# Attention on Trainium2: row maxima from 64-row tile pairs, latent scores in 2.5 passes, half the low-part subtractions on GpSimd

## The chip, the cores and the metric

One core of one Trainium2 chip runs the whole layer as one program. The time is the device time in microseconds of one execution, as the median of several runs. All times below are of this core.

## The reference

The layer is h = x + W_out(concat[GQA(xn) * silu(g_A), MLA(xn) * silu(g_B)]) with xn = RMSNorm(x), for 2048 tokens of width 1024, in float32. Both mixers are bidirectional softmax attention over all 2048 keys:

```python
def one_block(qblk):
    s = jnp.einsum('bkgqd,bksd->bkgqs', qblk, k).astype(jnp.float32) * scale
    p = jax.nn.softmax(s, axis=-1).astype(v.dtype)
    return jnp.einsum('bkgqs,bksd->bkgqd', p, v)
```

GQA has 8 query heads and 2 key/value heads of dimension 64. The latent mixer (MLA) has 4 heads with keys of 96 (64 + 32 rotary) and values of 128. Queries and keys are RMS-normalised per head, with gains about eight times the usual, so scores are large and softmax is sharp: the row maximum must be taken off before exp.

## The kernel before

The program has three phases: phase1 (projections, norms, rotary, transposes; up to 598 us), phase2 (attention; up to about 1636 us) and phase3 (gates and output projection). The change touches phase2 alone.

Float32 accuracy comes from float16 pairs: every operand is a high half and a low half (what float16 leaves over). A score tile is a sum of products of halves, accumulated in PSUM. For GQA (64 dimensions) the high and the low half of a key lie in partitions 0 to 63 and 64 to 127 of ka_hl, and qa_hh holds the high half of the query twice, so one matmul gives high x (high + low); a second one (ka_h1, qa_lm, 66 rows) adds high key x low query and, through two more rows, takes off the row maximum. For latent heads (96 dimensions) it takes three matmuls (L1026 to L1028).

**Units and steps.** Queries come in blocks of 512. phase2 runs N = 16 rounds; a round has three units: a GQA unit of key head 0, a GQA unit of key head 1 and a latent unit (UNITS, L700), each 512 queries against all 2048 keys. A unit has STEPS = 8 steps of 256 keys, a round HALF = 24 steps. A step s does:
- PE: two score tiles of 128 keys x 512 queries into st[:, s % 2] (scores, L1005 to L1029).
- ACT: exp of the 1024 columns into p32 (L847, float32), then its float16 high half ph (L852). p32 has N32 = 4 slots, ph and pl have NP = 8.
- DVE: the low half pl = p32 - ph (lo, L891 to L897).
- PE: P V of the step three earlier (PVLAG = 3; pv, L1033 to L1061), high and low half of P against the values, into acc. The values carry a column of ones, which gives the denominator.

**Row maxima ahead.** The row maximum of a unit must be there before its first score. So PE computes the scores twice: once with queries in rows (128 queries x 512 keys, max_scores, L962 and L964, high halves; GQA with the key's low half as well), into one of the two banks of mx; DVE reduces them (reduce, L869), one bank or both at a time; sixteen such pieces make a unit. Then DVE reduces the partial maxima and splits them in two float16 numbers (max_done, L873 to L879), PE turns them into a row by a product with the unit matrix (turn, L975 to L981, output 2 columns wide), and DVE casts that row into the query operand (rows, L886, L888). The pieces run LEAD = 30 ahead of the scores; a hand-written list (PIECES_IN, L637) says how many of them each step carries (48 in a round), and PE puts them between its scores and its P V halves. A prologue does the first 30 before the first score.

**Ends of units.** ACT copies acc to acc_sb (copy_acc, L839) at the third step of the next unit, DVE takes the reciprocal of the denominators (L912) two steps on, and GpSimd (POOL) adds the two GQA halves (L818) and multiplies by the reciprocal (L827). SP stores the result and loads the operands (L729 to L801) in one queue: queries of the next round after each unit's scores (s_st), the latent max operands after the round's row maxima (s_mx), latent keys after the last scores, latent values after the last P V (s_pv).

PE's order within a step is fixed by the program: scores, then max pieces and turn, then P V. The waits that tie the engines are: scores s wait for exp s - 2; exp s waits for the subtraction s - 4; a max piece waits until the piece before the last is reduced (L958); P V waits for ph and pl of its step.

Of the kernel before, what the change touches and what calls it, by code (L numbers as in the profile page):

```python
# [19 lines left out]
F16 = mybir.dt.float16  # L20
ALU = mybir.AluOpType
# [3 lines left out]
P = 128  # L25
# [11 lines left out]
QB = 512  # L37
# [588 lines left out]
def phase2(nc, QA, KA, QBd, KBd, VA, VB, YA, YB, w_out, w_raw):  # L626
# [8 lines left out]
    PIECES_IN = [2, 2, 2, 0, 2, 2, 2, 0] + [2, 2, 0, 2, 2, 2, 0, 2] + [2, 3, 3, 3, 3, 2, 4, 4]  # L637
    ROUND = 3 * PIECES
    pieces_of = lambda s: list(range(LEAD + sum(PIECES_IN[:s]), LEAD + sum(PIECES_IN[:s + 1])))
    KW = 2 * QB  # L640
    ONE = 64.0
    with ExitStack() as ctx:
# [19 lines left out]
        part = sb("part", [P, 2, PIECES])  # L662
# [21 lines left out]
        s_mx = sem("max_scores")  # L684
        s_red = sem("max_reduced")
# [6 lines left out]
        s_lo = sem("p_lo")  # L692
# [13 lines left out]
        def turned(s, last):  # L706


            for e in pieces_of(s - 1) if s else ():
                if e % PIECES == 3 and not (last and e // PIECES > 3):  # L710
                    return e
            return None

        def before(i, s, act_on, first):

            pos = s // STEPS - 1
            act_on(i if pos >= 0 else i - 1, pos % 3, first and pos == 0)
# [10 lines left out]
        def _(sp):  # L728
            def load_q(i, pos):  # L729
# [34 lines left out]
            for g in range(GA):  # L764
                for s, dsts in ((0, (ka_hl[g][0:64, :], ka_h1[g][0:64, :])), (1, (ka_hl[g][64:128, :],))):
# [586 lines left out]
```

## Time and profile before

| | us |
|---|---|
| median of 3 runs | 1847.05 |
| lowest, highest | 1846.85, 1848.38 |
| span of the profiled execution | 1847.9 |
| busy: PE, DVE, ACT, POOL | 1672.5, 1333.0, 1167.0, 61.6 |
| attention phase, first max matmul to last copy | 606.2 to 1633.3 |

The profile is of one execution, whose own time is given by its span alone. PE is TensorE (matmuls), PEld its weight loads, DVE VectorE, ACT ScalarE, POOL GpSimd, SP the queue that issues DMAs. Ends of matmuls are modelled, so start-to-start distances say more of PE than busy time. "Idle before" is the engine's idle time ahead of a row and what released it. The granted TensorE clock (PEclk) is a share of 2.4 GHz.

### The profile page before, as it was taken

Reading aid. Unit: us, or ns where it says so; the run is one execution under the profiler, and the core shown is the slowest. Engines: PE = TensorE matmul, PEld = TensorE weight load, DVE = VectorE, ACT = ScalarE, POOL = GpSimd, SP = SyncE. Lnnn points to the kernel's source line nnn. Section 1 sums busy time; section 2 is a strip of 40 time slices with the busy share of each in tenths; the row PEclk is TensorE's granted clock in tenths of the full one; section 3 lists DMA queues with packets and bytes.
Section 4 is the critical chain, followed back from the end, with each engine's and each line's share of the span. In section 5 each row is a group of like instructions: output and inputs, shape, how many; then the busy total and the mean of one; then the engine's idle time right before and its main releaser. Section 6 shows DMA issues by size and latency. Waiting matters only on the chain. (4 is left out here: it accounts for less than half of the span.)

```text
span 1847.9 us, 39666 instructions
## 1 busy us (share of the span) xinstructions
PE 1672.5 (91%) x14416; PEld 1003.5 (54%) x14416; DVE 1333.0 (72%) x1829; ACT 1167.0 (63%) x1506; POOL 61.6 (3%) x92
## 2 busy tenths in 40 slices
PE   4599999999994499999999999999999999959999
PEld 2355555555553056656665666666656665634444
DVE  4644545445463599999999999999999999842332
ACT  5445444454443088778877877887788778953332
POOL 0000000000000000000000000000000000000000
PEclk8799999999997599999999999999999999979999
DMA  6312302212221802212221222122212221235553
GB/s 215 108 46 65 95 32 82 77 51 77 63 71 52 209 23 62 68 44 53 58 68 36 62 57 65 35 68 57 65 31 72 57 61 34 54 100 165 173 174 126
DMA packets 202876, 143.54 MB, mean 78 GB/s; under 512 B 43216, under 2 KB 186064, under 8 KB 202832
## 3 DMA queue, kind: packets, MB, share of 16 engines
q1 hardware_dynamic: 202832, 142.94, 27.6%
q8 instruction: 29, 0.48, 0.1%
q14 instruction: 15, 0.12, 0.0%
HBM read 100.94 MB, written 41.97 MB: 77 GB/s over the span
## 5 line engine op out<-in xcount | busy, mean ns | idle before, releaser
L847 ACT ACTIVATE p_p<-p_st 128x1024 f32<-128x1024 f32 x384 | 390.2, 1016 | 210.5 <-PE p_st L1028 127.1
L869 DVE TENSOR_REDUCE p_part<-p_mx 128x1 f32<-128x512 f32 (+1 forms) x564 | 479.7, 878 | 38.0 <-PE p_mx L962 33.0
L896 DVE TENSOR_TENSOR p_pl<-p_p,p_ph 128x1024 f16<-128x1024 f32 x384 | 466.6, 1222 | 13.5 <-ACT p_ph L852 11.6
L515 PE MATMUL p_ring<-p_w_hi,p_xT 128*128 128x512 f16 (+3 forms) x1536 | 393.4, 343 | 34.2 <-issue 18.9
L852 ACT ACTIVATE p_ph<-p_p 128x1024 f16<-128x1024 f32 x384 | 405.8, 1057 | 16.6
L515 PE MATMUL p_ring<-p_w_lo,p_xT 128*128 128x512 f16 (+3 forms) x768 | 263.3, 343 | 0.0
L515 PEld LDWEIGHTS p_ring<-p_w_hi,p_xT 128*128 128x128 f16 x1536 | 152.1, 99 | 154.5 <-issue 42.8
L962 PE MATMUL p_mx<-p_ka_hl,p_qa_hh 128*128 128x512 f16 x512 | 190.3, 397 | 49.9 <-DVE p_part L869 28.5
L1053 PE MATMUL p_acc<-p_vas,p_ph 128*128 128x129 f16 x2048 | 219.7, 221 | 15.0 <-ACT p_acc_sb L839 15.0
L1054 PE MATMUL p_acc<-p_vas,p_pl 128*128 128x65 f16 x2048 | 211.0, 193 | 0.0
L1053 PEld LDWEIGHTS p_acc<-p_vas,p_ph 128*128 128x128 f16 x2048 | 183.6, 97 | 44.8 <-ACT p_acc_sb L839 22.9
L1054 PEld LDWEIGHTS p_acc<-p_vas,p_pl 128*128 128x128 f16 x2048 | 182.3, 98 | 29.0
L1024 PE MATMUL p_st<-p_qa_lm,p_ka_h 66*128 66x512 f16 x512 | 195.2, 381 | 0.0
L1023 PE MATMUL p_st<-p_qa_hh,p_ka_hl 128*128 128x512 f16 x512 | 194.8, 380 | 0.0
L1057 PE MATMUL p_acc<-p_vbs,p_ph 128*128 128x129 f16 x1024 | 184.9, 219 | 1.6 <-ACT p_acc_sb L839 1.6
L1059 PE MATMUL p_acc<-p_vbs,p_pl 128*128 128x129 f16 x1024 | 185.3, 222 | 0.0
L1058 PE MATMUL p_acc<-p_vbs,p_ph 128*128 128x128 f16 x1024 | 184.8, 219 | 0.0
L1302 PE MATMUL p_po<-p_w_hi,p_yT 128*128 128x512 f16 x512 | 159.0, 383 | 9.9 <-DVE p_res L1252 5.4
L962 PEld LDWEIGHTS p_mx<-p_ka_hl,p_qa_hh 128*128 128x128 f16 x512 | 48.0, 98 | 127.7 <-DVE p_part L869 90.7
L393 DVE COPY p_xT<-p_xtp 128x1024 f16<-128x1024 f16 x32 | 20.7, 686 | 133.4 <-PE p_xtp L539 133.4
L1057 PEld LDWEIGHTS p_acc<-p_vbs,p_ph 128*128 128x128 f16 x1024 | 100.9, 99 | 15.5 <-ACT p_acc_sb L839 2.1
L1058 PEld LDWEIGHTS p_acc<-p_vbs,p_ph 128*128 128x128 f16 x1024 | 98.7, 96 | 16.7
(136 smaller groups left out, 2158.2 us busy)
## 6 DMA issues: line engine op xcount, KB each, us to landing
p_vbs<-scratch_vb SPq DMA_DIRECT2D x16, 1028.0 KB, 6.1
p_xin<-in_x SPq DMA_DIRECT2D x16, 512.0 KB, 3.7
scratch_g<-p_g SPq DMA_DIRECT2D x16, 512.0 KB, 3.2
p_gt<-scratch_g SPq DMA_DIRECT2D x16, 512.0 KB, 4.8
p_xr<-in_x SPq DMA_DIRECT2D x16, 512.0 KB, 4.3
out<-p_res SPq DMA_DIRECT2D x16, 512.0 KB, 3.0
p_w_raw<-in_w_in SPq DMA_DIRECT2D x3, 2048.0 KB, 8.3
p_kb_m<-scratch_kb SPq DMA_DIRECT2D x16, 384.0 KB, 3.9
```

Source lines behind the costliest of these rows:

```text
L515: last = pe.matmul(ring[n % 3][:, 0:w], a, b, start=(m == 0), stop=(m == len(terms) - 1))
L847: act.activation(p32[:, s % N32, :], st[:, s % 2, :, :].rearrange("p a b -> p (a b)"), ACT.Exp, scale=scale).then_inc(s_exp, 1)
L852: act.activation(ph[:, s % NP, :, :].rearrange("p a b -> p (a b)"), p32[:, s % N32, :], ACT.Copy).then_inc(s_hi, 1)
L869: dve.tensor_reduce(part[:, upar, c:c + n], mx[:, c % 2:c % 2 + n, :], AX, ALU.max).then_inc(s_red, n)
L896: dve.tensor_tensor(pl[:, s % NP, :, :].rearrange("p a b -> p (a b)"), p32[:, s % N32, :], ph[:, s % NP, :, :].rearrange("p a b -> p (a b) ...
L962: pe.matmul(mx[:, c % 2, :], qa_hh[g][:, queries], ka_hl[g][:, keys], start=True, stop=True).then_inc(s_mx, 1)
L1023: pe.matmul(out, ka_hl[g][:, keys], qa_hh[g][:, :], start=True, stop=False)
L1024: end = pe.matmul(out, ka_h1[g][:, keys], qa_lm[g][:, :], start=False, stop=True)
L1053: pe.matmul(a, hi, vas[:, t, g, :], start=new, stop=False, skip_group_check=True)
L1054: last = pe.matmul(a[:, DA:], lo, vas[:, t, g, DA:], start=False, stop=end, skip_group_check=True)
L1057: pe.matmul(a, hi, vbs[:, t, DVB:], start=new, stop=False, skip_group_check=True)
L1058: pe.matmul(a[:, 0:DVB], hi, vbs[:, t, 0:DVB], start=False, stop=False, skip_group_check=True)
```

## The change

- Row maxima: a piece is now a pair (two key blocks of 512, both banks of mx), 8 pairs (MPAIRS) a unit; every step carries one, 10 ahead (LEAD), and DVE reduces both banks at once. PE issues a pair only when the pair before it is reduced. For GQA the pair takes high halves alone, 64 rows each: one matmul in partitions 0 to 63 (ka_hl), the other in 64 to 127 (a new copy of the keys, ka_up).
- Latent scores: the three products of 96 dimensions are packed in two matmuls of 128 rows and one of 34 rows (kb_1, kb_2, kb_3; qb_1, qb_2, qb_3); the 34-row ones of a step's two tiles lie in partitions 0 to 33 and 64 to 97. The turned row maxima of a latent unit go to two places, by 8 matmuls and two casts. Loads: 6 DMAs for the latent keys and 6 for the queries, where it was 2 and 2.
- Low halves: even steps on DVE, odd steps on GpSimd; ph and pl have 12 slots.
- DVE's order in a step: reduce; in odd steps then the subtraction of the step before. In a turn step: rows, then the reduction. The turns are in steps 6, 14 and 22; PE puts P V between the turn and that step's pair.
- P V: written as six halves late (PV_CARRY), which is three steps, in every step.

```diff
-    N32, NP = 4, 8
-    PVLAG = 3
...
-    LEAD = 30
-    PIECES_IN = [2, 2, 2, 0, 2, 2, 2, 0] + [2, 2, 0, 2, 2, 2, 0, 2] + [2, 3, 3, 3, 3, 2, 4, 4]
...
+    N32, NP = 4, 12
+    MPAIRS = 8
+    LEAD = 10
+    PV_HALVES = [2] * HALF
+    PV_CARRY = 6
+    COPY_AT = {2: -1, 10: 0, 18: 1}
+    TURN_AT = {6: 1, 14: 2, 22: 3}
...
-                for s, dst in enumerate((kb_h1[0:DB, :], kb_l[:, :])):
+                for dst, s, r0, r1 in ((kb_1[0:96, :], 0, 0, 96), (kb_1[96:128, :], 1, 0, 32),
+                                       (kb_2[0:64, :], 1, 32, 96), (kb_2[64:128, :], 0, 0, 64),
+                                       (kb_3[0:32, :], 0, 64, 96), (kb_3[64:96, :], 0, 64, 96)):
+                    src = KBd[s, h].rearrange("pr r t -> r pr t")[r0:r1]
+                    sp.dma_start(dst.rearrange("r (pr t) -> r pr t", pr=PAIRS), src).then_inc(s_kb, 16)
...
+            def lo(i, s, first):
+                n = i * HALF + s
+                pool.wait_ge(s_hi, n + 1)
+                if not (first and s < NP):
+                    pool.wait_ge(s_pv, n + 1 - NP)
+                pool.tensor_tensor(pl[:, s % NP, :, :].rearrange("p a b -> p (a b)"), p32[:, s % N32, :],
+                                   ph[:, s % NP, :, :].rearrange("p a b -> p (a b)"), ALU.subtract).then_inc(s_lop, 1)
+            def body(i, first, last):
+                for s in range(1, HALF, 2):
+                    lo(i, s, first)
+                    for at, pos in COPY_AT.items():
+                        if s == at + 1 - at % 2:
+                            unit_of(i, pos, unit, first)
+            loop(pool, body)
+            unit(N - 1, 2, False)
...
-                dve.tensor_reduce(part[:, upar, c:c + n], mx[:, c % 2:c % 2 + n, :], AX, ALU.max).then_inc(s_red, n)
+            def reduce(i, e):
+                upar, c = e // MPAIRS % 3 % 2, e % MPAIRS
+                dve.wait_ge(s_mx, i * HALF + e + 1)
+                dve.tensor_reduce(part[:, upar, 2 * c:2 * c + 2], mx[:, :, :], AX, ALU.max).then_inc(s_red, 1)
+                if c == MPAIRS - 1:
+                    max_done(i * 3 + e // MPAIRS, upar)
...
-                    dve.tensor_copy(qb_lm[DB:DB + 2, :], mx[DB:DB + 2, 0, :]).then_inc(s_mr, 1)
+                    dve.tensor_copy(qb_3[32:34, :], mx[32:34, 0, :])
+                    dve.tensor_copy(qb_3[96:98, :], mx[96:98, 0, :]).then_inc(s_mr, 1)
...
             def body(i, first, last):
                 for s in range(HALF):
+                    ahead = not (last and s + LEAD >= HALF)
+                    turn = TURN_AT.get(s) if not (last and s in TURN_AT and TURN_AT[s] > 2) else None
                     if turn is not None:
+                        rows(i * 3 + turn, turn % 3)
+                    elif ahead:
+                        reduce(i, s + LEAD)
+                    if s % 2 == 1:
                         lo(i, s - 1, first)
+                    if turn is not None and ahead:
+                        reduce(i, s + LEAD)
+                    if s - 1 in COPY_AT:
+                        unit_of(i, COPY_AT[s - 1], denominator, first)
...
+            def max_pair(i, e, start):
+                pos, c = e // MPAIRS, e % MPAIRS
+                g, kind = UNITS[pos % 3]
                 if not start:
+                    pe.wait_ge(s_red, i * HALF + e)
+                if c == 0:
+                    loaded(i + pos // 3, pos % 3)
+                queries = slice(c // 2 * P, (c // 2 + 1) * P)
+                for x in range(2):
+                    k0 = (c % 2 * 2 + x) * QB
+                    keys = slice(k0, k0 + QB)
+                    if kind == "a":
+                        rows, k = (slice(0, 64), ka_hl[g]) if x == 0 else (slice(64, 128), ka_up[g])
+                        mm = pe.matmul(mx[:, x, :], qa_hh[g][rows, queries], k[rows, keys], start=True, stop=True)
+                    else:
+                        mm = pe.matmul(mx[:, x, :], qb_m[:, queries], kb_m[:, keys], start=True, stop=True)
+                mm.then_inc(s_mx, 1)
...
                 pe.wait_ge(s_md, u * 3 + 3)
-                for j in range(QT):
-                    last = pe.matmul(mx[p0:p0 + 2, 0, j * P:(j + 1) * P], mpair[:, pos % 2, j, :], eye[:, :],
-                                     start=True, stop=True)
+                for p0 in ((64,) if kind == "a" else (32, 96)):
+                    for j in range(QT):
+                        last = pe.matmul(mx[p0:p0 + 2, 0, j * P:(j + 1) * P], mpair[:, pos % 2, j, :], eye[:, :],
+                                         start=True, stop=True, skip_group_check=True)
...
-                        pe.matmul(out, kb_h1[0:DB, keys], qb_h[:, :], start=True, stop=False)
-                        pe.matmul(out, kb_l[:, keys], qb_h[:, :], start=False, stop=False)
-                        end = pe.matmul(out, kb_h1[:, keys], qb_lm[:, :], start=False, stop=True)
+                        pe.matmul(out, kb_1[:, keys], qb_1[:, :], start=True, stop=False)
+                        pe.matmul(out, kb_2[:, keys], qb_2[:, :], start=False, stop=False)
+                if kind == "b":
+                    for b, r0 in ((0, 0), (1, 64)):
+                        k0 = (s % STEPS * 2 + b) * P
+                        end = pe.matmul(st[:, s % 2, b, :], kb_3[r0:r0 + 34, k0:k0 + P], qb_3[r0:r0 + 34, :],
+                                        start=False, stop=True)
...
+                v = -PV_CARRY
                 for s in range(HALF):
+                    ahead = not (last and s + LEAD >= HALF)
+                    turning = s in TURN_AT and not (last and TURN_AT[s] > 2)
+                    scores(i, s, first)
+                    if turning:
+                        turn(i * 3 + TURN_AT[s], TURN_AT[s] % 3)
+                    elif ahead:
+                        max_pair(i, s + LEAD, False)
+                    for _ in range(PV_HALVES[s]):
+                        if not (first and v < 0):
+                            pv(i, v, first)
+                        v += 1
+                    if turning and ahead:
+                        pe.wait_ge(s_mr, i * 3 + TURN_AT[s] + 1)
+                        max_pair(i, s + LEAD, False)
...
```

The helper loaded (waits for the operands) and unit (POOL, ends of units) are as before but for their order; GpSimd's unit work now comes after its subtraction of step 3, 11 or 19.

## Rows read from the trace of the kernel before

**Rows 1.** The page, busy time: us, share of the span, instructions of each engine.

```profile
PE 1672.5 (91%) x14416; PEld 1003.5 (54%) x14416; DVE 1333.0 (72%) x1829; ACT 1167.0 (63%) x1506; POOL 61.6 (3%) x92
```

**Rows 2.** Timeline of ACT: start us, us, engine, line, op, out<-in, count.

```profile
1023.67 0.58 ACT L839 ACTIVATE p_acc_sb<-p_acc 128x516 f32<-128x516 f32 x1
1026.28 1.00 ACT L847 ACTIVATE p_p<-p_st 128x1024 f32<-128x1024 f32 x1
1051.68 1.02 ACT L847 ACTIVATE p_p<-p_st 128x1024 f32<-128x1024 f32 x1 [0.33 <-PE p_st L1028]
1085.74 0.58 ACT L839 ACTIVATE p_acc_sb<-p_acc 128x516 f32<-128x516 f32 x1
...
1632.74 0.60 ACT L839 ACTIVATE p_acc_sb<-p_acc 128x516 f32<-128x516 f32 x1 [3.39 <-PE p_acc L1059]
```

**Rows 3.** Busy time by stretch: stretch, us, engines, granted clock, DMA share, GB/s.

```profile
997.18:1059.24 62.06, 59.95 (x621) 37.94 (x620) 60.24 (x76) 50.20 (x52) 3.72 (x5) 1.00 0.23 56
1023.67:1040.52 16.85, 16.38 (x179) 9.93 (x176) 16.45 (x17) 16.39 (x19) 1.04 (x1) 1.00 0.35 90
```

**Rows 4.** Timeline of PE and DVE in GQA steps, then latent P V.

```profile
1025.97 0.60 PE L964 MATMUL p_mx<-p_kb_m,p_qb_m 96*128 96x512 f16 x2
1026.67 1.22 DVE L869 TENSOR_REDUCE p_part<-p_mx 128x2 f32<-128x1024 f32 x1 [0.23 <-PE p_mx L964]
1027.10 0.38 PE L1023 MATMUL p_st<-p_qa_hh,p_ka_hl 128*128 128x512 f16 x1
1027.97 0.60 PE L964 MATMUL p_mx<-p_kb_m,p_qb_m 96*128 96x512 f16 x2
1029.10 0.38 PE L1023 MATMUL p_st<-p_qa_hh,p_ka_hl 128*128 128x512 f16 x1
...
1060.67 0.22 PE L1059 MATMUL p_acc<-p_vbs,p_pl 128*128 128x129 f16 x1
1060.84 0.22 PE L1059 MATMUL p_acc<-p_vbs,p_pl 128*128 128x129 f16 x1
```

**Rows 5.** Timeline of DVE, a subtraction and a double reduction.

```profile
1035.92 1.21 DVE L896 TENSOR_TENSOR p_pl<-p_p,p_ph 128x1024 f16<-128x1024 f32 x1
1037.05 1.21 DVE L869 TENSOR_REDUCE p_part<-p_mx 128x2 f32<-128x1024 f32 x1
```

**Rows 6.** Timeline of DVE, the last reduction of a unit and what follows.

```profile
1016.64 1.23 DVE L869 TENSOR_REDUCE p_part<-p_mx 128x2 f32<-128x1024 f32 x1 [0.55 <-PE p_mx L962]
1018.50 1.23 DVE L896 TENSOR_TENSOR p_pl<-p_p,p_ph 128x1024 f16<-128x1024 f32 x1
```

**Rows 7.** Timeline of PE and DVE around a turn, and around a cast.

```profile
1023.76 0.38 PE L1024 MATMUL p_st<-p_qa_lm,p_ka_h 66*128 66x512 f16 x1
1024.08 0.39 PE L979 MATMUL p_mx<-p_eye,p_mpair 128*2 128x128 f16 x4
1024.39 0.23 PE L1053 MATMUL p_acc<-p_vas,p_ph 128*128 128x129 f16 x1
...
1048.16 0.70 DVE L888 CAST p_qb_lm<-p_mx 2x512 f16<-2x512 f32 x1
1048.91 0.22 PEld L962 LDWEIGHTS p_mx<-p_ka_hl,p_qa_hh 128*128 128x128 f16 x2 [0.21 <-DVE p_qb_lm L888]
```

**Rows 8.** Timeline of POOL and DVE where a subtraction and a POOL operation meet.

```profile
1615.80 1.22 DVE L896 TENSOR_TENSOR p_pl<-p_p,p_ph 128x1024 f16<-128x1024 f32 x1 [0.77 <-ACT p_ph L852]
...
1599.84 0.74 POOL L818 TENSOR_TENSOR p_ysum<-p_acc_sb 128x256 f32<-128x256 f32 x1 [10.79 <-ACT p_acc_sb L839]
1616.33 1.28 POOL L818 TENSOR_TENSOR p_ysum<-p_acc_sb 128x256 f32<-128x256 f32 x1 [12.28 <-ACT p_acc_sb L839]
...
1029.34 1.04 POOL L827 TENSOR_TENSOR p_yout<-p_acc_sb,p_rden 128x512 f32<-128x512 f32 x1 [23.30 <-DVE p_rden L912]
...
1030.15 1.31 DVE L896 TENSOR_TENSOR p_pl<-p_p,p_ph 128x1024 f16<-128x1024 f32 x1
```

**Rows 9.** Timeline of the prologue, the weight load of a row-max pair.

```profile
608.57 0.13 PEld L962 LDWEIGHTS p_mx<-p_ka_hl,p_qa_hh 128*128 128x128 f16 x2 [2.29 <-DVE p_part L869]
```

More of the change, by code:

```diff
@@ L704, in y_before, with lo_done, unit_of @@
             return i * 5 + 2 * pos
[L706 to L717, printed above, removed]
+        def lo_done(eng, i, s):
+            if s % 2 == 0:
+                eng.wait_ge(s_lo, i * (HALF // 2) + s // 2 + 1)
+            else:
+                eng.wait_ge(s_lop, i * (HALF // 2) + s // 2 + 1)
+        def unit_of(i, pos, act_on, first):
+            if pos < 0:
+                if not first:
+                    act_on(i - 1, 2, False)
+            else:
+                act_on(i, pos, first and pos == 0)
         def loop(eng, body):
@@ L821, in unit @@
                 else:
[L822 removed]
                     src = acc_sb[:, :, 0:w]
                 pool.wait_ge(s_rden, u + 1)
[L825 removed]
+                if not first:
                     pool.wait_ge(s_yst, u * 16)
@@ L828, in unit @@
                                    ALU.mult).then_inc(s_y, 1)
-            loop(pool, lambda i, first, last: [unit(i, pos, first) for pos in range(3)])
+            def lo(i, s, first):
[13 more added lines that the diff above has]
+            unit(N - 1, 2, False)
         @block.scalar
@@ L856, in body @@
                     step(i, s, first)
-                    if s % STEPS == PVLAG - 1 and not (first and s < STEPS):
-                        before(i, s, copy_acc, first)
+                    if s in COPY_AT:
+                        unit_of(i, COPY_AT[s], copy_acc, first)
             loop(act, body)
@@ L1016, in scores @@
                 for b in range(2):
-                    if b == 1 and between is not None:
-                        ahead(i, between, last)
                     k0 = (s % STEPS * 2 + b) * P
@@ L1075, in body @@
-                    scores(i, s, first, last, at(0)[0] if at(0) else None)
-                    turn_step(i, s, last)
-                    for e in at(1):
-                        ahead(i, e, last)
-                    for b in range(2):
-                        if not (first and s < PVLAG):
-                            pv(i, s - PVLAG, first, b)
-                        for e in at(2 + b):
-                            ahead(i, e, last)
-            pe.wait_ge(s_eye, 2)
-            pe.wait_ge(s_const, 3)
```

162 lines of the change are left out of this document (47 added, 115 removed).

## The prediction

> **What bounds the kernel now.** I read the page's totals first, then the copies of the accumulator, which mark the rounds, then busy time by stretch, then single steps. The totals [rows 1] show PE busy 91% and DVE 72% of the span: an average over three phases, which decides nothing. The copies [rows 2] mark the attention phase: one round of 24 steps takes 62.07 us (1023.67 to 1085.74), there are 16, and the last copy ends at 1632.74 + 0.60 = 1633.3. Within a round [rows 3] DVE is busy 60.24 of 62.06 us, PE 59.95, ACT 50.20. PE's figure holds modelled ends; its pace says more [rows 4]: four 512-column matmuls start in 0.87 us (1027.10 to 1027.97), 0.217 each, though each lasts 0.38. A step of 2.00 (1027.10 to 1029.10) is four for scores, two for row maxima and 0.70 for P V; a latent P V is 8 x 0.17 = 1.36. A round is then 48 x 0.217 = 10.4 (row maxima), 112 x 0.217 = 24.3 (scores), 16 x 0.70 + 8 x 1.36 = 22.1 (P V) and 0.9 (turns): 57.7 us. So DVE is the tighter engine over the round, and between 1023.67 and 1040.52 ACT is (16.39 of 16.85 [rows 3]); its pace there is 2.00 a step.
>
> **DVE's work.** A 1024-column operation on DVE repeats every 1.13 us [rows 5]. Twelve subtractions leave each round: 13.6 us. The single reductions become doubles (about 0.8 less), and a second cast for the latent unit comes in (0.73). DVE's work falls from 60 to about 46.5 us. The round need not shrink with it, because the order changes.
>
> **The new loop.** mx holds one pair, and PE may issue the next only once DVE has reduced it. Before, a subtraction followed every double reduction and covered the next pair. Now DVE runs reduce (even step), reduce (odd step), subtract, and nothing covers PE between the two reductions. By the rows: a pair's first matmul to its reduction 0.70 (1025.97 to 1026.67), reduction's start to PE's next pair 1.30 (1026.67 to 1027.97) [rows 4], and 1.13 each for the two DVE operations between. Two steps take 0.70 + 1.13 + 1.13 + 1.30 = 4.26 us, above ACT's 4.00 and above PE's own work. What is late next: behind the waiting pair stand P V and the following scores in PE's order, ACT waits for those, and as this recurs in every pair of steps no look-ahead averages it out.
>
> **Turn steps.** The max chain now lies ahead of the subtraction in the step before a turn: from reduction to subtraction 1.86 [rows 6]. The subtraction takes 1.24 to the cast, the cast 0.75 to PE's next pair [rows 7]; that pair now comes only after the cast. All of it is serial: 0.70 + 1.86 + 1.24 + 0.77 + 0.70 + 1.30 = 6.57 us for the two steps, 7.30 with the latent unit's second cast. The turn and P V lie beside it.
>
> **PE.** The two halves of a GQA pair (64 rows each), and the last passes of two latent score tiles (34 rows each), can run at once. No row shows two matmuls at once. Bounds for two: 0.217 (wholly at once) and 0.433 (one after the other). I take 0.297: the second one 0.08 behind the first, by a weight load. Going from whole-array to half-array work isn't in the trace either; nearest is the turn, whose output is two columns wide: 1023.76 to 1024.08 is 0.32 where 0.22 is usual, and its four 128-column matmuls hold PE 0.31 (to 1024.39) for 0.22 of columns [rows 7]. So 0.10 in, 0.09 out; bounds 0 and 0.163 (0.38 less 0.217, a full run-out). A GQA pair then costs 0.10 + 0.297 + 0.09 = 0.49, where it cost 0.433: no gain. A latent step's scores and pair cost 0.867 + 0.10 + 0.297 + 0.267 + 0.09 = 1.62, against 1.95: this is what the change wins on PE.
> The page TensorEngine Tiling of the Trainium skill (Key Properties) says that a change of tiling mode drains the engine; at the upper bound that is 1.6 us more a round. The page TensorE: Matmul & The Clock Gate of the Trainium skill (Part 3) has tiles start about 4 ns apart, by estimate 0.08 less per pair. No row here shows either.
>
> **Sum of a round.** P V runs three steps late before and after, so steps 0 to 2 carry the latent P V and 16 to 18 a GQA one.
> Steps 0-1: PE, 2 x (0.867 + 0.49 + 1.36) = 5.43. 2-3: 2.72 + 2.06 = 4.78. 4-5: 4.26. 6-7: 6.57. Reciprocal 0.1. Together 21.1.
> Steps 8 to 13: 3 x 4.26. 14-15: 7.30. Reciprocal 0.1. Together 20.2.
> Steps 16-17: 2 x 2.32 = 4.64. 18-19: 5.30. 20-21: 2 x 2.98 = 5.96. 22-23: PE, with the turn, reaches the even pair at 4.85, + 0.70 + 1.30 = 6.85. Together 22.7.
> A round is 64.0 us, against 62.07. What is won after step 16 is lost in steps 4 to 15: 30.9 by this sum, 25.4 before (exp of step 4 at 1026.28, of step 16 at 1051.68 [rows 2]).
>
> **GpSimd.** Its product of 512 columns takes 1.04 us [rows 8], so at least 1.9 for 1024; its sum of two full tensors is 0.73 for 256, so at most 2.9. I take 2.4, as the new operation is like the sum, with a fixed part paid once. It has 4.26 us for each and P V comes three steps later: the time alone costs nothing. The two engines are in each other's way, though. A GpSimd sum issued at 1616.33, inside a DVE subtraction (1615.80 to 1617.02), took 1.28 instead of 0.73 and ended 0.56 after it; a subtraction issued 0.23 before the end of a GpSimd product took 1.31 instead of 1.22 [rows 8]. Whoever comes second waits for the other's end. In ordinary pairs of steps DVE subtracts 1.83 to 3.05 us after the odd pair; GpSimd's input is ready at 0.19 + 1.05 + 1.06 + about 0.15 = 2.45, it runs 3.05 to 5.3, and DVE's next comes at 6.1: no clash. Before a turn DVE's subtraction begins at 0.70 + 1.86 = 2.56: a dead heat with 2.45. If GpSimd wins, cast and pair are about 2.1 us late. Bounds a round: 0 and 3 x 2.1 less 0.2. I take one lost race of three, 2.1, since DVE's operations stand ready in its queue while GpSimd must wake. The round is 66.1.
> The page GPSIMD Engine Reference of the Trainium skill (3.1) gives 4497 ns for 2048 float32 columns on GpSimd and 2293 on DVE; by that ratio an estimate is 1.22 x 1.96 = 2.4.
>
> **Ahead, behind, DMA.** The prologue reduces 10 pairs, not 15, each 2.42 us (2.29 idle before a pair's first load, 0.13 the load) [rows 9]: 12.1 less. One more memset and one more key copy ahead of it, and the turn's own place, give back 2.6: 9.5 less. The last round costs 4.7 more (it loses less to loops, and ends behind a GpSimd subtraction, 0.7), 6 with its race. SP issues 8 more DMAs a round (latent queries and keys) of 0.3 to 0.6 us; the keys have some 35 us until step 16, and the DMA engines are 23% busy [rows 3]: nothing. Without that cover 5 us a round. The y stores, vbs and the max operands stand behind them with tens of us to spare.
> Sum: 15 x (66.1 - 62.07) = 60, + 6 - 9.5 = +57. The profiled execution's span is 1847.9, 0.9 over the median 1847.05: on the median it makes 1904.
>
> **Rivals.**
> Faster (0.22): halves run wholly at once, switches are free, GpSimd loses every race. Steps 0 to 7 take 4.89 + 4.22 + 4.04 + 6.35 + 0.1, the others 19.9 and 20.3: 59.8. 15 x (-2.2) - 11 = -44, 1804; with one race lost a round 1838. For it: no row excludes these ends. Against: the loops rest on known prices.
> Slower still (0.17): GpSimd is first before all three turns. It decides once its operand is ready ahead of DVE's 2.56. Round 64.0 + 6.1 = 70.1, time + 121 + 6 - 9.5: 1965. For it: both rows of the collision. Against: it needs the race lost thrice.
> Halves don't run at once and switches run out (0.10): GQA steps 2.33, latent ones 2.76 and 3.42, round 69.0: 1945.
> No change (0.03): errors cancel, or PE holds step pace so that neither loop nor gain shows.
>
> **How the numbers follow.** Forecast (0.48): round 64 to 68, 1870 to 1935, likeliest 1904. The range leaves out the better half of the faster case and the rest of the all-lost one: 1828 to 1968. A measurement of this kernel can tell about 0.2% (3.7 us) from no change. Faster 0.22, same 0.03, slower 0.75.
>
> **What would show it.** Copies of one unit 64 to 68 us apart. DVE idle about 0.9 before every second reduction, behind PE's max pair; DVE 70% busy in a round; ACT idle in steps 4 to 15, where it was full. The halves of a pair under 0.1 apart, 0.10 lost on either side. GpSimd subtractions about 2.4, longer when started behind DVE's; DVE subtractions over 3 us just before a turn, where a race was lost. I am wrong if steps 8 to 13 take 4.0 a pair, or if the round is under 62.

## The result, and the profile after

The changed kernel takes 1876.01 us (median of 4 runs, 1873.92 to 1879.41), the kernel before beside it 1847.28 (4 runs): ratio 1.0156, 95% interval 1.0142 to 1.0171. It is slower by 28.7 us where the forecast had 57; the direction is right, and 1876 lies in the range, below its centre. The profiled execution has a span of 1872.7, 3.3 us under this median. The page of the kernel after, totals, granted clock and costliest groups (to be held against [rows 1]):

```profile
PE 1664.7 (89%) x14480; PEld 954.7 (51%) x14480; DVE 1128.2 (60%) x1474; ACT 1170.1 (62%) x1506; POOL 560.4 (30%) x284
...
PEclk9799999999996699999999999999999999979999
...
L841 POOL TENSOR_TENSOR p_pl<-p_p,p_ph 128x1024 f16<-128x1024 f32 x192 | 500.2, 2605 | 494.4 <-ACT p_ph L874 491.1
L891 DVE TENSOR_REDUCE p_part<-p_mx 128x2 f32<-128x1024 f32 x384 | 469.4, 1222 | 266.4 <-PE p_mx L973 200.2
...
L921 DVE TENSOR_TENSOR p_pl<-p_p,p_ph 128x1024 f16<-128x1024 f32 x192 | 236.2, 1230 | 13.4 <-ACT p_ph L874 13.1
```

DVE lost 205 us of work and the kernel became slower: DVE now idles 266 us ahead of its reductions, 200 of them behind PE's GQA pairs.

**Where it went.** The first score starts at 626.58 us (642.29 before), the last copy ends at 1657.9 (1633.3 before). So the prologue wins 15.7, and the rounds lose about 40. A round falls into three stretches by its copies: steps 2 to 10, 10 to 18, and 18 to step 2 of the next round. Busy time of one round by these stretches (columns: length, then busy us and instructions of PE, PEld, DVE, ACT, POOL, then PEclk, DMA share, GB/s). The kernel after, in the order 18 to 2, 2 to 10, 10 to 18:

```profile
998.60:1021.75 23.15, 22.49 (x253) 14.57 (x250) 15.62 (x17) 17.02 (x18) 11.58 (x7) 1.00 0.33 70
1021.75:1041.15 19.40, 17.71 (x184) 9.80 (x182) 15.41 (x17) 16.54 (x19) 11.16 (x5) 1.00 0.35 86
1041.15:1063.94 22.79, 20.60 (x194) 10.44 (x192) 16.22 (x18) 16.81 (x19) 11.99 (x7) 0.85 0.14 36
```

The same of the kernel before, in the order 2 to 10, 10 to 18, 18 to 2 (the stretch 18 to 2 is the latent one, the other two are the GQA ones):

```profile
1023.67:1040.52 16.85, 16.38 (x179) 9.93 (x176) 16.45 (x17) 16.39 (x19) 1.04 (x1) 1.00 0.35 90
1040.52:1059.24 18.72, 17.58 (x183) 10.90 (x184) 18.52 (x24) 16.68 (x18) 1.34 (x2) 1.00 0.16 44
1059.24:1085.74 26.50, 26.00 (x262) 17.11 (x260) 25.27 (x38) 17.13 (x18) 1.34 (x2) 1.00 0.20 42
```

The latent stretch wins 3.35 us; the GQA stretches lose 2.55 and 4.07. Not all of the 3.35 is packing: PE issues 22 row-max pieces in that stretch before and 16 after, and six pieces of 0.217 us are 1.3 us that went into the GQA stretches. And one column has changed that the prediction never used: the granted clock is 0.85 in the third stretch of after. Over 14 rounds the mean is 64.6 us ((1603.82 - 699.00) / 14 by the copies), before 62.06.

**The loops are there as forecast.** DVE in steps 8 to 13 of after:

```profile
1033.21 1.23 DVE L891 TENSOR_REDUCE p_part<-p_mx 128x2 f32<-128x1024 f32 x1 [0.70 <-PE p_mx L975]
1034.35 1.22 DVE L921 TENSOR_TENSOR p_pl<-p_p,p_ph 128x1024 f16<-128x1024 f32 x1
1035.49 1.22 DVE L891 TENSOR_REDUCE p_part<-p_mx 128x2 f32<-128x1024 f32 x1
1037.40 1.23 DVE L891 TENSOR_REDUCE p_part<-p_mx 128x2 f32<-128x1024 f32 x1 [0.70 <-PE p_mx L975]
```

Two steps take 4.19 (forecast 4.26; 1033.21 to 1037.40). Before every second reduction DVE stands idle for 0.70 while PE computes the pair, and no other DVE operation covers it. ACT needs 4.00.

**The clock falls.** PE of after at the latent turn, which is the turn of step 14, with row maxima for the latent unit; those of steps 6 and 22 are the GQA turns (a step's later P V products left out), and the windows around it:

```profile
1047.98 0.40 PE L991 MATMUL p_mx<-p_eye,p_mpair 128*2 128x128 f16 x8 [0.35 <-DVE p_mpair L902]
1048.31 0.23 PE L1046 MATMUL p_acc<-p_vas,p_ph 128*128 128x129 f16 x1
...
1050.72 0.60 PE L973 MATMUL p_mx<-p_ka_hl,p_qa_hh 64*128 64x512 f16 x1 [1.54 <-DVE p_qb L913]
1050.73 0.60 PE L973 MATMUL p_mx<-p_ka_up,p_qa_hh 64*128 64x512 f16 x1
1051.27 0.61 PE L1013 MATMUL p_st<-p_qa_hh,p_ka_hl 128*128 128x512 f16 x1
1051.67 0.63 PE L1014 MATMUL p_st<-p_qa_lm,p_ka_h 66*128 66x512 f16 x1
```

```profile
1049.00:1050.00 1.00, 0.18 (x5) 0.03 (x2) 0.95 (x3) 0.86 (x1) 1.00 (x1) 1.00 0.15 30
1050.00:1051.00 1.00, 0.28 (x2) 0.11 (x2) 0.48 (x1) 0.00 (x0) 1.00 (x1) 0.72 0.00 0
1051.00:1052.00 1.00, 1.00 (x4) 0.28 (x3) 0.63 (x1) 0.00 (x0) 0.04 (x1) 0.50 0.00 0
...
1057.00:1058.00 1.00, 1.00 (x15) 0.48 (x12) 0.36 (x1) 0.52 (x1) 1.00 (x1) 0.87 0.64 180
```

PE waits 1.54 us for the second cast, and right behind it the clock stands at 0.50, the level of 1.2 GHz, until about 1057.5: matmuls start 0.40 to 0.43 apart, not 0.22. The first fourteen rounds of after have fifteen such falls, of 3 to 7 us each: ten behind the latent turn (steps 10 to 18 then take 21.0 to 22.8, otherwise 20.24), five behind a GQA one (steps 2 to 10 then take 21.0 to 21.5, otherwise 19.40). Before, the windows of 120 us from 760 to 1600 all have 1.00.

The length of the wait does not decide alone. The same 1.54 us stand at every latent turn, and one round earlier no fall follows it; there the fall came 20 us sooner, behind a GQA turn where PE had waited 0.95 us (windows of 1 us from 968: 0.76, 0.50, 0.50, 0.53).

```profile
966.28 0.60 PE L975 MATMUL p_mx<-p_kb_m,p_qb_m 96*128 96x512 f16 x2 [0.95 <-DVE p_qa_lm L910]
987.94 0.38 PE L973 MATMUL p_mx<-p_ka_hl,p_qa_hh 64*128 64x512 f16 x1 [1.54 <-DVE p_qb L913]
```

```profile
989.00:990.00 1.00, 0.66 (x5) 0.13 (x4) 0.59 (x1) 0.66 (x1) 0.00 (x0) 1.00 0.00 0
```

### The profile page after: what moved, and what is told of

It is laid out like the page before. It is cut to its first block and busy times, and to the rows that moved or that the text cites. A ratio compares the mean times of both kernels' runs of the same rounds, so it can differ in the third digit from the quotient of the medians.

```text
span 1872.7 us, 38858 instructions
## 1 busy us (share of the span) xinstructions
PE 1664.7 (89%) x14480; PEld 954.7 (51%) x14480; DVE 1128.2 (60%) x1474; ACT 1170.1 (62%) x1506; POOL 560.4 (30%) x284
## 5 line engine op out<-in xcount | busy, mean ns | idle before, releaser
L841 POOL TENSOR_TENSOR p_pl<-p_p,p_ph 128x1024 f16<-128x1024 f32 x192 | 500.2, 2605 | 494.4 <-ACT p_ph L874 491.1
L891 DVE TENSOR_REDUCE p_part<-p_mx 128x2 f32<-128x1024 f32 x384 | 469.4, 1222 | 266.4 <-PE p_mx L973 200.2
L921 DVE TENSOR_TENSOR p_pl<-p_p,p_ph 128x1024 f16<-128x1024 f32 x192 | 236.2, 1230 | 13.4 <-ACT p_ph L874 13.1
L1046 PE MATMUL p_acc<-p_vas,p_ph 128*128 128x129 f16 x2048 | 224.4, 226 | 5.0 <-ACT p_acc_sb L861 4.8
L1014 PE MATMUL p_st<-p_qa_lm,p_ka_h 66*128 66x512 f16 x512 | 202.1, 395 | 0.0
L1013 PE MATMUL p_st<-p_qa_hh,p_ka_hl 128*128 128x512 f16 x512 | 201.1, 393 | 0.0
L1047 PEld LDWEIGHTS p_acc<-p_vas,p_pl 128*128 128x128 f16 x2048 | 187.6, 100 | 12.2 <-issue 1.2
L973 PE MATMUL p_mx<-p_ka_hl,p_qa_hh 64*128 64x512 f16 x256 | 104.0, 406 | 58.1 <-DVE p_qb L913 22.9
L1050 PEld LDWEIGHTS p_acc<-p_vbs,p_ph 128*128 128x128 f16 x1024 | 100.9, 99 | 47.0 <-issue 43.3
L515 PEld LDWEIGHTS p_ring<-p_w_lo,p_xT 128*128 128x128 f16 x768 | 76.0, 99 | 57.9 <-issue 3.1
```

What stands on the lines that cost most here:

```text
L515: last = pe.matmul(ring[n % 3][:, 0:w], a, b, start=(m == 0), stop=(m == len(terms) - 1))
L841: pool.tensor_tensor(pl[:, s % NP, :, :].rearrange("p a b -> p (a b)"), p32[:, s % N32, :], ph[:, s % NP, :, :].rearrange("p a b -> p (a b ...
L891: dve.tensor_reduce(part[:, upar, 2 * c:2 * c + 2], mx[:, :, :], AX, ALU.max).then_inc(s_red, 1)
L921: dve.tensor_tensor(pl[:, s % NP, :, :].rearrange("p a b -> p (a b)"), p32[:, s % N32, :], ph[:, s % NP, :, :].rearrange("p a b -> p (a b) ...
L1013: pe.matmul(out, ka_hl[g][:, keys], qa_hh[g][:, :], start=True, stop=False)
L1014: end = pe.matmul(out, ka_h1[g][:, keys], qa_lm[g][:, :], start=False, stop=True)
```

## Experiments

Beside these kernels the kernel before took 1847.8 to 1848.3 us. The stretches of a round, by the copies of one round near 1050 us:

| kernel | time | ratio to before | 2 to 10 | 10 to 18 | 18 to 2 | round |
|---|---|---|---|---|---|---|
| before | 1847.3 | | 16.85 | 18.72 | 26.50 | 62.07 |
| after | 1876.0 | 1.0142 to 1.0171 | 19.40 | 22.79 | 23.15 | 65.34 |
| a_warm | 1850.2 | 1.0005 to 1.0024 | 19.40 | 20.27 | 23.16 | 62.83 |
| a_split | 1952.7 | 1.0528 to 1.0593 | 22.61 | 22.26 | 23.45 | 68.32 |
| a_dvelo | 1906.9 | 1.0294 to 1.0398 | 20.25 | 21.73 | 23.36 | 65.34 |
| b_pool | 1849.6 | 1.0000 to 1.0019 | 16.92 | 18.18 | 27.11 | 62.21 |
| a_gqa128w | 1956.4 | 1.0567 to 1.0603 | 22.74 | 20.98 | 25.54 | 69.26 |
| a_seqw | 1894.3 | 1.0235 to 1.0269 | 19.40 | 21.50 | 24.66 | 65.56 |
| b_lat | 1867.9 | 1.0092 to 1.0125 | 16.84 | 19.31 | 27.01 | 63.16 |
| a_skip | 1857.4 | 1.0036 to 1.0070 | 17.75 | 20.27 | 25.00 | 63.02 |
| h_pack_pool | 1864.7 | 1.0068 to 1.0109 | 16.84 | 18.98 | 27.52 | 63.34 |
| h_pack | 1886.7 | 1.0189 to 1.0224 | 16.85 | 19.93 | 28.10 | 64.88 |
| h_nopack_pool | 1869.7 | 1.0097 to 1.0135 | 16.85 | 19.07 | 27.87 | 63.79 |
| a_skip2 | 1846.0 | 0.9975 to 0.9999 | 17.75 | 18.97 | 25.21 | 61.93 |

One round is not the mean where the clock falls in some rounds and not in others: over 14 rounds the mean is 64.63 in after, 69.68 in a_split, 66.30 in a_dvelo and 69.62 in a_gqa128w. The others are within 0.2 of the table.

**a_warm: dummy matmuls hold the clock.**

```diff
                     if turning and ahead:
+                        if s in (14,):
+                            for _ in range(7):
+                                pe.matmul(mx[:, 1, :], qa_hh[1][:, 0:P], ka_hl[1][:, 0:QB], start=True, stop=True)
                         pe.wait_ge(s_mr, i * 3 + TURN_AT[s] + 1)
```

> The changed kernel, with 7 extra 512-column matmuls (1.5 us of dummy work, results never read) in the latent turn step, just ahead of PE's wait for the cast rows (1.54 us idle now). Theory K: the granted clock no longer falls to 0.56-0.59 behind that wait; 7 us at half speed a round go, worth 2 to 3 us a round, time 1830 to 1850. Theory L: the clock costs nothing that is not hidden, time 1876 to 1885, as the dummy work is at best free.

Measured 1850.2, 26 us faster than the changed kernel, by adding work whose results are never read. PE at the same place:

```profile
1040.47 1.67 PE L1073 MATMUL p_mx<-p_ka_hl,p_qa_hh 128*128 128x512 f16 x7
1042.21 0.38 PE L973 MATMUL p_mx<-p_ka_hl,p_qa_hh 64*128 64x512 f16 x1
1042.22 0.39 PE L973 MATMUL p_mx<-p_ka_up,p_qa_hh 64*128 64x512 f16 x1
1042.53 0.39 PE L1013 MATMUL p_st<-p_qa_hh,p_ka_hl 128*128 128x512 f16 x1
```

The pair comes no earlier behind the turn (2.78 us from the turn's start, 1039.43 to 1042.21; in the changed kernel 2.74), but what follows runs at full pace. Steps 10 to 18 fall from 22.79 to 20.27. One fall is left of the fifteen (1338 to 1342). So the fall of the clock is a cause, and it costs about 26 us in all. What is left, 62.83 against 62.07, is the loops and turns less the latent gain.

**a_dvelo: all subtractions back on DVE.**

```diff
-                    if s % 2 == 1:
+                    if not (first and s == 0):
                         lo(i, s - 1, first)
```

> The changed kernel, with all subtractions back on DVE, one behind every reduction. Theory L: every pair is covered, but DVE now paces at 2.26 a step (4.52 in two steps against 4.19), turn steps 6.8 against 6.6; the round grows by some 1.5 us, time near 1900. Theory C: collisions with GpSimd are gone; if they had cost 2.1 us a round as forecast, this wins them back and the time stays at or under 1876.

Measured 1906.9: theory L, to 7 us. Its clock falls as well (0.96 to 1.00 in windows of 120 us, eleven falls), so this run still holds a cost of that kind. Taking GpSimd away does not help. Of DVE's 192 subtractions in the changed kernel only one took over 3 us (3.18, issued at 1359.29, inside a fall of the clock), one took 1.61, the median is 1.216. So collisions cost DVE next to nothing there.

**a_split: the subtraction in two halves, one behind each reduction.**

```diff
+                    if ahead:
+                        reduce(i, s + LEAD)
                     if s % 2 == 1:
-                        lo(i, s - 1, first)
+                        lo(i, s - 1, 0, first)
+                    elif not (first and s == 0):
+                        lo(i, s - 2, 1, first)
```

> The changed kernel, with each DVE subtraction cut in two halves of 512 columns, one behind each row-max reduction, so that something covers every max pair. Theory L (the uncovered pair and the serial turn steps make the round 64.8 us): the loop of two steps falls from 4.19 to below ACT's 4.00, the turn steps from 6.6 to about 6.0, the round to about 62.3, time near 1838. Theory K (the fall of TensorE's clock to 0.56-0.59 behind the latent turn makes the difference to the kernel before): the wait of 1.54 us ahead of the fall gets only 0.6 shorter, the fall stays, gain under 15 us, 1862 or more. Theory C (the two engines that share SBUF get in each other's way): shorter DVE operations collide more often, no gain.

Measured 1952.7: no theory had a loss of 77 us; C's "no gain" comes nearest. The order lets GpSimd start first, and then even DVE's 4-column step of the max chain waits for it:

```profile
1061.09 2.12 POOL L841 TENSOR_TENSOR p_pl<-p_p,p_ph 128x1024 f16<-128x1024 f32 x1 [0.58 <-ACT p_ph L874]
1061.19 2.04 DVE L902 SCALAR_TENSOR_TENSOR p_mpair<-p_rowmax,p_mpair 128x4 f16<-128x4 f32 x1
...
1063.29 0.38 PE L992 MATMUL p_mx<-p_eye,p_mpair 128*2 128x128 f16 x4 [1.81 <-DVE p_mpair L902]
```

That step takes 0.17 when alone; its mean is 748 ns over the rounds here. The reductions, with their one operand in PSUM, keep their 1222 ns. The page SBUF — State Buffer of the Trainium skill (SBUF: two separate sides) says that a DVE operation with two SBUF inputs and a GpSimd operation that reads SBUF exclude one another, whoever starts first; these rows agree, down to the 4-column operation. How the 77 us divide among held operations and the clock (0.91 to 0.96 in windows of 120 us) was not taken apart.

**b_pool: the kernel before with GpSimd's half of the subtractions alone.**

```diff
-                    if not (first and s == 0):
+                    if s % 2 == 1:
                         lo(i, s - 1, first)
```

> The kernel before, with one thing of the change alone: the subtractions of odd steps on GpSimd. DVE falls from 60 to about 47 us a round, PE's own work is 57.7. Theory L: three steps of four hold a double reduction in two thirds of the round, so an uncovered pair now and then finds slack (6 x 1.13 + 4 x 1.13 + turn in 8 steps of 2.00), and the round becomes PE's and ACT's: 58.5 to 59.5, time 1790 to 1808. Theory C: collisions eat 2 us a round of that: 1820 or more.

Measured 1849.6, no gain where 40 to 58 us were expected. Its round by stretches (2 to 10, 10 to 18, 18 to 2):

```profile
1023.99:1040.91 16.92, 16.11 (x179) 9.97 (x177) 12.37 (x12) 16.34 (x19) 10.43 (x6) 1.00 0.34 89
1040.91:1059.09 18.18, 17.43 (x184) 10.91 (x185) 14.76 (x21) 16.69 (x18) 11.55 (x7) 1.00 0.16 43
1059.09:1086.20 27.11, 25.74 (x261) 17.06 (x260) 21.96 (x32) 17.13 (x18) 10.11 (x6) 1.00 0.19 42
```

DVE went from 60.25 to 49.09 us of 62.2, and only the second stretch is shorter, by 0.54. The last is 0.61 longer, and the trace shows a collision in it, in fifteen of the sixteen rounds. GpSimd holds up a 4-column step of the max chain, the reductions behind it come 1.3 late, and PE waits for a bank of mx where it did not wait before:

```profile
1062.11 2.13 POOL L839 TENSOR_TENSOR p_pl<-p_p,p_ph 128x1024 f16<-128x1024 f32 x1 [3.50 <-ACT p_ph L871]
1062.80 1.46 DVE L895 TENSOR_SCALAR p_mpair<-p_rowmax 128x4 f16<-128x4 f32 x1
1065.14 0.39 PE L980 MATMUL p_mx<-p_ka_hl,p_qa_hh 128*128 128x512 f16 x1 [0.96 <-DVE p_part L888]
```

So "no gain" is a small gain less this wait of 0.96. Without it the round would be near 61.3 by estimate (62.21 less 0.96), still far above the 58.5 to 59.5 expected. DVE's load did not bound the kernel before over the round. By their busy times the first stretch is ACT's (16.34 of 16.92) and the last PE's (25.74 of 27.11); no run tested this by taking work from either alone.

**b_lat: the kernel before with the packed latent scores alone** (kb_1 to kb_3, qb_1 to qb_3, the turn to two places, as in the change).

> The kernel before, with one thing of the change alone: latent scores in two full passes and one of 34 rows that runs for both tiles at once. By the prices of the trace 0.87 + 0.10 + 0.22 + 0.09 = 1.28 takes the place of 1.30 a step: no gain, 1844 to 1852 (a second cast of 0.7 us a round lies under ACT's pace). Rival: a change of mode costs nothing, then 0.19 a step and 1.6 a round in the stage that PE bounds: 1823.

Measured 1867.9: it costs 20 us. Steps 10 to 18 are 0.59 longer, the stretch where DVE was busy 18.52 of 18.72 and where the second cast now stands (19.10 of 19.31). The latent stretch is 0.51 longer and not shorter. Why was not taken apart; PE waits 0.53 there for a reduced bank (at 1078.30) where it waited 0.20 before (at 1070.06).

**a_seqw and a_gqa128w: what runs at once, taken apart.** Both carry the dummy matmuls of a_warm.

```diff
 # a_seqw
-                for b, r0 in ((0, 0), (1, 64)):
...
+                        r0 = 64 * b
+                        end = pe.matmul(out, kb_3[r0:r0 + 34, keys], qb_3[r0:r0 + 34, :], start=False, stop=True)
 # a_gqa128w
-                        rows, k = (slice(0, 64), ka_hl[g]) if x == 0 else (slice(64, 128), ka_up[g])
-                        mm = pe.matmul(mx[:, x, :], qa_hh[g][rows, queries], k[rows, keys], start=True, stop=True)
+                        mm = pe.matmul(mx[:, x, :], qa_hh[g][:, queries], ka_hl[g][:, keys], start=True, stop=True)
```

> The changed kernel with the dummy matmuls that hold the clock (1850 us), and the two 34-row last passes of a latent step each right behind the two full passes of their own tile, so they no longer run at once. By the prices 0.22 for one pass, 0.10 into the half-array mode and 0.09 out of it, each latent step takes 0.41 more, eight steps a round, all in the stage that PE bounds: round + 3.3, time near 1900. If a change of mode costs nothing of its own: + 0.22 a step, 1876.

Measured 1894.3, 44 above a_warm, 2.73 a round. A latent step on PE, from its first score to that of the next step, first in a_warm, then in a_seqw:

```profile
1047.17 0.38 PE L1016 MATMUL p_st<-p_qb,p_kb 128*128 128x512 f16 x1
1049.38 0.38 PE L1016 MATMUL p_st<-p_qb,p_kb 128*128 128x512 f16 x1
```

```profile
1061.94 0.39 PE L1019 MATMUL p_st<-p_qb,p_kb 34*128 34x512 f16 x1
1061.95 0.39 PE L973 MATMUL p_mx<-p_ka_hl,p_qa_hh 64*128 64x512 f16 x1
1063.19 0.38 PE L1016 MATMUL p_st<-p_qb,p_kb 128*128 128x512 f16 x1
1065.83 0.38 PE L1016 MATMUL p_st<-p_qb,p_kb 128*128 128x512 f16 x1
```

2.21 became 2.64 (2.88 became 3.30 in steps with latent P V): 0.42 a step, and 0.41 was expected. 0.22 is the pass, so the added pair of mode changes costs 0.20, as in the trace. The round grows by 0.34 a step and not 0.42, so some of it lies off PE's path. The second 34-row pass still found a partner: it starts 0.01 before the first half of the max pair, in other rows.

> The changed kernel with the dummy matmuls that hold the clock (1850 us), and its GQA max pairs again in 128 rows (products with the key's low half too), so that the two matmuls of a pair run one behind the other. Theory H (the halves of a pair run wholly at once, 0.22 for two, and pay 0.19 for the mode changes): in a latent step, where the pair stands beside the half-array last passes and shares their mode, it costs 0.43 for 0.22; elsewhere 0.43 for 0.41 and the reduction starts 0.2 later. Six to eight steps by 0.22 and some loops by 0.2: the round grows by 2.0 to 2.5, time 1880 to 1888. If halves gain nothing (rival), 1850.

Measured 1956.4, far above both. With GQA pairs 0.2 us longer on PE, the race that the prediction described goes the other way. DVE and GpSimd before a turn, in a_gqa128w:

```profile
1059.42 0.17 DVE L902 SCALAR_TENSOR_TENSOR p_mpair<-p_rowmax,p_mpair 128x4 f16<-128x4 f32 x1
1059.61 3.16 DVE L921 TENSOR_TENSOR p_pl<-p_p,p_ph 128x1024 f16<-128x1024 f32 x1
1062.80 0.69 DVE L910 CAST p_qa_lm<-p_mx 2x512 f16<-2x512 f32 x1
```

```profile
1059.56 2.13 POOL L841 TENSOR_TENSOR p_pl<-p_p,p_ph 128x1024 f16<-128x1024 f32 x1 [0.72 <-ACT p_ph L874]
```

GpSimd is first by 0.05 us, DVE's subtraction takes 3.16 for 1.22, and PE waits 2.89 for the cast. In the changed kernel DVE is ahead at this turn by 0.28 us (1028.48 against 1028.76), and before the latent turn by 0.07:

```profile
1047.84 1.22 DVE L921 TENSOR_TENSOR p_pl<-p_p,p_ph 128x1024 f16<-128x1024 f32 x1
```

```profile
1047.91 3.13 POOL L841 TENSOR_TENSOR p_pl<-p_p,p_ph 128x1024 f16<-128x1024 f32 x1 [0.50 <-ACT p_ph L874]
```

There GpSimd, with three steps of slack, pays. Over the phase of a_gqa128w DVE loses 30 times: 13 subtractions take over 2 us, and 17 times the 4-column step of the max chain does, as here:

```profile
1035.99 2.13 DVE L902 SCALAR_TENSOR_TENSOR p_mpair<-p_rowmax,p_mpair 128x4 f16<-128x4 f32 x1
```

Two races a round at 2 us each are some 60 of the 106 us over a_warm, by estimate. How the rest divides between the 0.2 itself and the clock (0.96 or 0.97 in six of eight windows of 120 us, in spite of the dummy matmuls) was not taken apart; in one round the clock goes to 0.50 right behind the wait of 2.89.

**a_skip and a_skip2: no pair in a turn step.**

```diff
-    LEAD = 10
+    LEAD = 12
+    PAIRS_IN = [1, 1, 1, 1, 0, 1, 1, 1] + [1, 1, 1, 1, 1, 0, 1, 1] + [1, 2, 2, 1, 0, 2, 1, 1]
-    TURN_AT = {6: 1, 14: 2, 22: 3}
+    TURN_AT = {4: 1, 13: 2, 20: 3}
 # a_skip2: [1, 1, 1, 2, 1, 0, 2, 2] in the latent steps, turn 3 in step 21,
 # the turns of steps 4 and 13 behind P V, and the pair of the next step too
```

> The changed kernel, with no max pair in the three turn steps (moved to steps 4, 13 and 20) and three pairs more in latent steps instead; pairs run 12 ahead, not 10. Theory L+K: with no pair waiting for the cast rows the serial turn steps (6.57 us for two steps) go, and with them the wait of 1.54 us and the fall of the clock behind it. Steps 2 to 9 take 17.0 to 17.5 (19.40 now), 10 to 17 18.0 to 18.5 (22.79 now, 20.27 with the clock held), the latent stage about 24.4 (23.16 now, for three more mode changes and pairs of 0.41): round 59.5 to 60.3, time 1800 to 1815. If the loops of two reductions are the larger part and the turns the smaller (L alone), the round stays at 61.5 or more, 1830 or more.

Measured 1857.4. The clock is 0.99 to 1.00 without any dummy work, with two falls left. Steps 2 to 10 take 17.75, near the forecast of 17.0 to 17.5; steps 10 to 18 (20.27) and the latent stretch (25.00) are well above theirs. The time is on the side of "L alone", 1830 or more: with its clock held the kernel is 7 us slower than a_warm.

> As a_skip (no max pair in a turn step, three double steps), with what its trace shows waiting taken out: the turns of steps 4 and 13 stand behind both P V halves, and so does the next step's pair (a_skip: PE waited 0.74 us for the chain and 1.02 for the casts); the double steps are 19, 22 and 23, where the latent P V of 1.36 us lies between the two pairs (a_skip: 0.5 to 0.6 waited before each second pair). If single waits of PE behind the one buffer of row-max scores are what is left (theory L), steps 10 to 17 fall from 20.27 to about 18.5 and the latent stage from 25.0 to 24.3: round near 60.5, time 1815 to 1825, faster than both kernels. If a wait taken away only comes back at the next reduction, since each pair of steps holds two reductions and two uncovered pairs in series, the round stays above 62, 1840 or more.

Measured 1846.0 (10 runs), ratio to the kernel before 0.9987 (0.9975 to 0.9999): 30 us under the changed kernel, and level with the one before, within what a measurement can tell. 26 of the 30 are what a_warm wins by the clock alone; the new order adds 4. Steps 10 to 18 gave 1.30 of the 1.77 expected, the latent stretch none. With a single buffer of row-max scores every second reduction still waits for its pair; DVE of a_skip2:

```profile
1023.75 1.21 DVE L893 TENSOR_REDUCE p_part<-p_mx 128x2 f32<-128x1024 f32 x1
1025.66 1.22 DVE L893 TENSOR_REDUCE p_part<-p_mx 128x2 f32<-128x1024 f32 x1 [0.70 <-PE p_mx L977]
1026.80 1.22 DVE L923 TENSOR_TENSOR p_pl<-p_p,p_ph 128x1024 f16<-128x1024 f32 x1
1027.93 1.22 DVE L893 TENSOR_REDUCE p_part<-p_mx 128x2 f32<-128x1024 f32 x1
```

**h_pack_pool, h_pack, h_nopack_pool: the order of the kernel before with the means of the change.**

```diff
-    PIECES_IN = ... [2, 3, 3, 3, 3, 2, 4, 4]
+    PIECES_IN = ... [2, 4, 4, 4, 2, 2, 2, 4]
-                    n = 2 if s < 2 * STEPS else 1
+                    n = 2
```

> The kernel before, with its own order (12 of 16 GQA steps carry a double max piece, the turn two steps behind the max chain) and all three means of the change laid into it: GQA max pieces in two 64-row halves, packed latent scores, odd subtractions on GpSimd. In the latent stage the 24 single pieces become 12 pairs, and a pair stands behind the 34-row passes in their mode. Theory L+H+K: before's order has no serial turn and no wait of 1.5 us, so the clock stays and the GQA stages keep 16.9 and 18.7 (with the second cast); the latent stage falls from 26.5 to 25.0. Round 60.6, prologue 7 less: time 1815 to 1825, faster than both kernels. Theory S (the three means bring nothing, and 23.16 in the changed kernel came from pairs moved out of the latent stage alone): latent stage 26.5 or more, time 1845 or more.

> The same without GpSimd: all subtractions on DVE. DVE then has 24.2 us of work in a latent stage of 25, and about 59 in a round. If DVE was never the bound of the kernel before (as its variant with half the subtractions on GpSimd says, 1849.6), this is within 5 us of the one with GpSimd. If DVE becomes the bound once PE has less to do, it is 10 us or more above it.

> The same as the first, without the packed latent scores (three full passes, one cast). Packing alone cost 1.1 us a round in the kernel before; with a pair behind it that shares the mode it should win 0.21 in six to eight steps and pay 0.6 for the cast: 0.6 to 1.1 a round, so this one is 10 to 16 us above the first. If sharing the mode brings nothing, this one is 10 to 16 us below it.

Measured 1864.7, 1886.7, 1869.7. The first GQA stretch stays at the 16.85 of before, as expected; the second is 18.98 and 19.07 with GpSimd and 19.93 without, against 18.72. The latent one is 27.5 to 28.1, not 25: theory S. h_nopack_pool differs from b_pool in having all pieces as pairs, in another list of them and in GQA halves, and it is 20 us slower. With single pieces, PE fills one bank of mx while DVE reduces the other; a pair takes both. That this is the price is the likely reading, but list and pair form were not changed apart. Neither halves nor packing repay it there. Without GpSimd it is 22 us worse, so DVE's share does matter once pieces are all pairs. Packing wins 0.35 in the latent stretch and 0.09 in the one before it, 5 us in all, where 10 to 16 were expected.

## Why the prediction was right, and where it was off

- **What bounds the kernel before.** "DVE is the tighter engine over the round": wrong. b_pool takes 11 us of work a round from DVE and gains nothing, or about 1 us if its collision is left out. The busy shares of a whole round hid three stretches which, by their busy times, have three limits: ACT, DVE by half a microsecond, and PE with its two banks. The forecast did not suffer, since it summed stage by stage.
- **The new loop.** 4.26 forecast, 4.19 measured; DVE idle 0.70 before every second reduction, 0.9 forecast; before, a subtraction stood there [rows 5]. With the turn it stretches steps 2 to 10 by 2.55.
- **Turn steps.** 6.57 forecast for a GQA turn, 6.58 measured (reductions at 1026.63 and 1033.21 us). For the latent turn 7.30 forecast, 6.82 with the clock held (a_warm, reductions at 1037.54 and 1044.35).
- **PE.** Two halves start 0.00 to 0.01 us apart (1050.72 and 1050.73 above), so two cost 0.22, the lower bound, where 0.297 was taken. The mode changes cost 0.09 in and 0.09 out in the trace, 0.10 and 0.09 forecast. A latent step's scores and pair take 1.50 (1000.89 to 1002.39), 1.62 forecast. The 1.95 that the prediction set against 1.62 holds three pieces, where the change has two: with two it is 1.74, so PE wins 0.24 a step and the third piece is only moved. The clock held, a round is 62.92 (14 rounds of a_warm) and not 64.0; 0.48 of that is the latent turn, and the halves are the nearest reason for the rest, being 0.08 in each of 16 GQA pairs and 8 latent steps, of which not all lie on the path. No run shows this division. The page TensorE: Matmul & The Clock Gate of the Trainium skill (Part 3) has tiles start about 4 ns apart; the rows agree.
- **GpSimd.** Its subtraction takes 2.13 us when it starts alone, inside the bounds of 1.9 and 2.9. The mechanism was right (whoever is second waits), and so was the place (a near dead heat before a turn: DVE ahead by 0.07 us before the latent one, by 0.28 at 1028.48). The term was mis-sized: 2.1 us a round for one lost race of three, where DVE lost one race in the whole phase. 30 us of the forecast are gone with it. (The GpSimd sum of [rows 8] ended 0.59 us after the subtraction, not 0.56; nothing hangs on it.) a_gqa128w shows two races of three lost a round; that its 1956 lies near the 1965 of the all-lost rival is chance, as it has longer pairs and falls of the clock besides.
- **The clock: no term at all.** The prediction noticed PE's wait at the turns and did not ask what it does to the clock. It costs 1.7 us a round (64.6 less 62.9).
- **The sum.** 66.1 forecast, less 2.1 for the races, less 1.1 for halves and the rest, plus 1.7 for the clock: 64.6, as measured. Two errors of near 30 us each with opposite signs stood in a forecast that came out right. This is luck: with its clock held the same kernel takes 1850 (a_warm), 3 us from the kernel before and 20 under the range. The prediction's own mechanism, at the sizes measured, gives next to no change; what makes the kernel slower by 26 of its 29 us is the term that the prediction did not have.
- **Ahead.** The prologue wins 15.7, not 9.5: a pair repeats every 1.93 us (DVE reductions at 607.32, 609.25, 611.18), 2.42 before [rows 9], since its two halves cost one pass less, 0.43 at the granted clock of 0.50 there. The last round costs 2.9, 5 to 6 forecast.
- **What held as told beforehand**: copies 64 to 68 us apart (mean 64.6); DVE 72% busy in a round (47.24 of 65.34), 70% forecast; latent stretch shorter, GQA stretches longer.

## What to carry to other kernels

Read the limit stage by stage, and test it by taking work from the engine that looks fullest: here 11 us a round came off DVE for nothing. When a producer and a consumer share one buffer, count the uncovered latency between two uses in series; a faster engine does not shorten it, a second bank or another operation in between can. In the kernel before the second bank does; of the orders tried here with an operation in between, none beat it. When work goes to GpSimd, look at the smallest DVE operations of the critical chain too: they are held as long as the large ones. And wherever TensorE is left waiting for about a microsecond, look at the granted clock of the stretch behind the wait: either remove the wait, or fill it with matmuls whose results are never read. Both were worth 19 to 30 us here.

## What was not expected of the hardware

- The granted clock goes to 0.50 (1.2 GHz) about a microsecond behind a wait of 1.54 us (three in some rounds) and stays there for up to 7 us (1050 to 1057.5); behind a wait of 0.95 us it does so for 3 to 4. Ten of fifteen equal waits of 1.54 us had a fall behind them; what decides was not found. Seven dummy matmuls in one turn step of three kept the clock at 0.99 to 1.00 in every window of 120 us, and so removed the falls behind the GQA turns as well, all but one. Why those went too stays open.
- A GpSimd subtraction of 2.12 us holds up a DVE operation of 4 columns for its whole length (0.17 alone, 2.04 behind it), and reductions out of PSUM not at all.
- Two matmuls in different rows start together though they belong to different products: a 34-row score pass in rows 64 to 97 and a 64-row max half in rows 0 to 63 (0.01 us apart, 1061.94 and 1061.95 in a_seqw).
- 0.2 us more on PE for each GQA pair turns races between two other engines: DVE loses 30 of them in a_gqa128w and one in the changed kernel, some 60 of the 106 us between 1850 and 1956 by estimate.
